# Two experts on two column halves of TensorE: units taken in turn, or matmul by matmul

## The reference, cut to what matters

```python
logits = (t @ w_router + b_router).astype(jnp.float32)
top_logit, top_idx = lax.top_k(logits, TOP_K)          # 4 of 32
...
xb = t_pad[rows]
gu = xb @ w_gate_up[e] + b_gate_up[e]                  # 1024 -> 2048
gate, up = jnp.split(gu, 2, axis=-1)
gate = jnp.minimum(gate, SWIGLU_LIMIT)
up = jnp.clip(up, -SWIGLU_LIMIT, SWIGLU_LIMIT)
act = (up + 1.0) * gate * jax.nn.sigmoid(SWIGLU_ALPHA * gate)
return act @ w_down[e] + b_down[e]                     # 1024 -> 1024
```

## Time and profile before

| what | value |
|---|---|
| median of 3 runs | 1329.62 us (1328.64 to 1331.16) |
| span of the profiled execution | 1325.7 us |
| PE busy | 1273.0 us, 96% |
| PEld busy | 720.2 us, 54% |
| DVE, ACT busy | 256.2 us, 174.9 us |
| read from HBM | 444.80 MB |
| the experts, from the first L657 to the end | 363.2 us to 1325.7 us |

### The profile page before, as it was taken

One profiled execution on the slowest core, in us unless ns is written; L12 is line 12 of the kernel. 1 busy time (PEld: TensorE's weight loads), 2 busy tenths in 40 slices (PEclk: granted clock), 3 DMA queues, 4 the chain that ended last, 5 costly groups with the idle time before them and its releaser, 6 DMA issues.

```text
span 1325.7 us, 14813 instructions
## 1 busy us (share of the span) xinstructions
PE 1273.0 (96%) x5921; PEld 720.2 (54%) x5921; DVE 256.2 (19%) x478; ACT 174.9 (13%) x297; POOL 0.9 (0%) x6
## 2 busy tenths in 40 slices
PE   8999999999899999999999999999999999999997
PEld 6878877888744535353444535353444535353443
DVE  2144221311302202020202202020202202020202
ACT  2233311100201101010101101010101101010100
POOL 0000000000000000000000000000000000000000
PEclk9999999999899999999999999999999999999999
DMA  9622332343698989999999999999999999999994
GB/s 381 259 96 95 112 111 95 130 157 133 264 375 351 367 352 414 420 417 417 418 415 421 414 422 414 420 415 419 418 416 419 415 422 415 421 415 420 416 416 166
DMA packets 78893, 446.29 MB, mean 337 GB/s; under 512 B 6896, under 2 KB 8048, under 8 KB 41232
## 3 DMA queue, kind: packets, MB, share of 16 engines
q1 hardware_dynamic: 78384, 443.64, 82.7%
q10 hardware_dynamic: 480, 2.23, 0.4%
HBM read 444.80 MB, written 1.05 MB: 336 GB/s over the span
## 4 chain that ended last, share of the span: by engine, by line
PE 89%; DVE 7%; issue 2%; ACT 1%; DMA 0%; DVEq 0%
PE ps L657 37%; PE ps L691 22%; PE ps L422 19%; DVE arena L1129 3%; PE ps L700 2%; PE ps L665 2%; DVE arena L1143 1%; DVE arena L1145 1%; DVE arena L1142 1%; ACT arena L898 1%; PE ps L495 1%; PE ps L463 1%; PE ps L431 1%; PE ps L677 0%; PE ps L638 0%
## 5 line engine op out<-in xcount | busy, mean ns | idle before, releaser
L657 PE MATMUL ps<-ring,arena 128*64 128x512 f32 x1984 | 472.4, 598 | 11.4 <-ACT arena L898 10.7
L657 PEld LDWEIGHTS ps<-ring,arena 128*64 128x64 f32 x1984 | 183.7, 136 | 297.9 <-issue 297.4
L691 PE MATMUL ps<-ring,arena 128*64 128x512 f32 x1008 | 285.1, 601 | 22.6 <-DVE arena L1145 22.6
L422 PE MATMUL ps<-arena,ring 128*128 128x256 f32 (+1 forms) x1184 | 268.9, 384 | 1.2 <-DVE arena L1044 1.1
L422 PEld LDWEIGHTS ps<-arena,ring 128*128 128x128 f32 x1184 | 222.0, 190 | 36.5 <-issue 5.0
L691 PEld LDWEIGHTS ps<-ring,arena 128*64 128x64 f32 x1008 | 100.2, 137 | 184.4 <-issue 158.7
L1136 DVE COPY arena<-ps 128x1024 f32<-128x1024 f32 x16 | 19.6, 1225 | 552.9 <-PE ps L657 552.9
L889 ACT ACTIVATE arena<-ps 128x1024 f32<-128x1024 f32 x16 | 16.4, 1024 | 472.6 <-PE ps L657 472.6
L638 PE MATMUL ps<-arena 128*128 128x128 f32 x512 | 63.2, 284 | 1.5 <-DVE arena L1129 1.5
L638 PEld LDWEIGHTS ps<-arena 128*128 128x128 f32 x512 | 60.8, 198 | 5.0 <-issue 5.0
L700 PE MATMUL ps<-arena 128*128 128x256 f32 x256 | 62.0, 386 | 0.0
(11 more groups left out here) (173 smaller groups left out, 493.5 us busy)
## 6 DMA issues: line engine op xcount, KB each, us to landing
ring<-in_w_gate_up SPq DMA_DIRECT2D x248, 1024.0 KB, 13.5
ring<-in_w_down SPq DMA_DIRECT2D x126, 1024.0 KB, 16.9
ring<-in_mix_w SPq DMA_DIRECT2D x37, 1024.0 KB, 4.9
arena<-in_w_gate_up SPq DMA_DIRECT2D x8, 1024.0 KB, 10.1
arena<-in_w_down SPq DMA_DIRECT2D x2, 1024.0 KB, 16.1
arena<-in_consts ACTq DMA_DIRECT2D x1, 1424.0 KB, 13.5
arena<-in_xT SPq DMA_DIRECT2D x2, 544.0 KB, 5.3
out<-arena SPq DMA_DIRECT2D x4, 256.0 KB, 2.6
```

The lines of the kernel that those rows point to most:

```text
L422: last = mm(ps[:, PROJ + half, 0:rhs.shape[-1]], w[:, k, half * P:(half + 1) * P], rhs, start=(k == 0), stop=(k == KC - 1))
L657: last = mm(ps[half, GATE + b], xeT[:, j, half], w[:, b * 512:(b + 1) * 512], start=(j == 0), stop=(j == 7))
L691: last = mm(ps[half, UP + b], e_act[:, k, half], w[:, f * D + b * 512:f * D + (b + 1) * 512], start=(k == 0), stop=(k == 7))
```

## The change

In `gate_up` and `down`, TensorE waits for both experts' units of a block at once, and then goes through the block's matmuls with the two experts alternating: bank 0 of expert 0, bank 0 of expert 1, bank 1 of expert 0, and so on. Each expert's last matmul of the block counts its unit as used. In `down` the count `first_half` moves with the matmul that it hangs on. The number of matmuls, their operands and their sums stay. SP, DVE, ACT and GpSimd have the same instructions in the same order as before.

```diff
-                for q in range(16):
-                    j, x = divmod(q, 2)
-                    w, half = unit_landed(n, q), slice(x * CAP, (x + 1) * CAP)
+                halves = (slice(0, CAP), slice(CAP, 2 * CAP))
+                for j in range(8):
+                    w = [unit_landed(n, 2 * j + x) for x in range(2)]
                     for b in range(4):
-                        last = mm(ps[half, GATE + b], xeT[:, j, half], w[:, b * 512:(b + 1) * 512],
-                                  start=(j == 0), stop=(j == 7))
-                    last.then_inc(units_used, 1)
+                        for x, half in enumerate(halves):
+                            last = mm(ps[half, GATE + b], xeT[:, j, half], w[x][:, b * 512:(b + 1) * 512],
+                                      start=(j == 0), stop=(j == 7))
+                            if b == 3:
+                                last.then_inc(units_used, 1)
...
-                for q in range(16, 24):
-                    if q == 22:
+                halves = (slice(0, CAP), slice(CAP, 2 * CAP))
+                for j in range(8, 12):
+                    if j == 11:
                         turn_weighted(n, last_pair)
-                    j, x = divmod(q, 2)
-                    w, half = unit_landed(n, q), slice(x * CAP, (x + 1) * CAP)
+                    w = [unit_landed(n, 2 * j + x) for x in range(2)]
                     for b in range(2):
                         for f in range(2):
                             k = 2 * (j - 8) + f
-                            last = mm(ps[half, UP + b], e_act[:, k, half],
-                                      w[:, f * D + b * 512:f * D + (b + 1) * 512], start=(k == 0), stop=(k == 7))
-                        if q == 23 and b == 0:
+                            for x, half in enumerate(halves):
+                                last = mm(ps[half, UP + b], e_act[:, k, half],
+                                          w[x][:, f * D + b * 512:f * D + (b + 1) * 512], start=(k == 0), stop=(k == 7))
+                                if b == 1 and f == 1:
+                                    last.then_inc(units_used, 1)
+                        if j == 11 and b == 0:
                             last.then_inc(first_half, 1)
-                    last.then_inc(units_used, 1)
```

## The result

The changed kernel takes 1317.31 us (median of 4 runs, 1316.01 to 1317.51) against 1329.13 us for the kernel before (4 runs, 1327.30 to 1331.16): a ratio of 0.9912, 95% interval 0.9900 to 0.9923, or 11.8 us less. Predicted were 1315.9 us, with a range of 1312.5 to 1321, and 13.7 us less. The profiled execution has a span of 1314.2 us, 11.5 less than before.

The account below looks back on a forecast made before the run. Transfers were taken as the slower side (60.2 us a pair, 0.6 more than TensorE), hidden by a stock of landed units. 10.0 us from earlier landings plus 3.7 from the last pair gave 13.7 less: 1315.9 us, range 1312.5 to 1321.

Parts of the forecast that it names:

- the landings: All later landings of weight units, behind the first pairs, come 10.0 us earlier (bounds 8.7 and 10.7).
- the last pair: Behind its last gate-up unit, the two `down` runs shorten by 2.0 and 1.7 us: 3.7 us less.
- The share of the halves: Alternating halves overlap from start to end: `gate_up` 27.7 us, `down` 10.55 and 3.66, a pair 6.2 us less of TensorE.
- The couple: One matmul of either half, run together: taken as 0.43 us, bounded below by 0.43 and above by 0.49.
- Rivals 1 and 2: Each change of half costs 0.05 us (1327 us, 8%); halves shut each other out (over 500 us slower, 4%).
- The middle pairs: Transfers take 60.2 us a pair, so TensorE's 6.2 us saved become waiting, about 1.3 us a block, worth nothing.
- The first pairs: Transfers stood still for 18.2 us while waiting for TensorE, the most that can come back there.
- The part from TensorE's runs: Shorter runs ahead of pair 1's first `down` unit end the last standstill of transfers 8.7 us earlier.
- the small gaps behind it: Behind the last standstill, up to 482 us, earlier freeing recovers 1.3 us (bounds 0 and 2).
- The slots: SP's 12 slots: freeing units two at a time, up to 1.7 us later, is covered; no new standstill arises.
- Rival 3: TensorE's 1.3 us waits in middle-pair blocks lower the clock to 1.2 GHz: 24 us, 1340 us; chance 5%.
- From span to median: The median of the runs lies 3.9 us above the profiled span, so 1312.0 us becomes 1315.9.

Follow-up runs that it names:

- the loop alone: Only pairs 2 to 14 alternate, the other pairs as in the kernel before: 1329.55 us against 1329.15, ratio 1.0003.
- the last pair alone: Only pair 15 alternates, the other pairs as in the kernel before: 1326.08 us against 1329.15, ratio 0.9975.
- The fill run: The changed kernel with 32 unread matmuls in the idle stretch ahead of the last pair's `down`: 1314.81 us, ratio 0.9897 to the kernel before.
- groups of two: The changed kernel, each expert taking two matmuls (four in the trace) before the other's turn: 1316.86 us, ratio 0.9900 to the kernel before.
- first pairs alone: Only pairs 0 and 1 alternate, the other pairs as in the kernel before: 1321.17 us against 1329.15, ratio 0.9940.
- half bytes, units in turn: The kernel before, with half the bytes in each unit in pairs 2 to 15: 1328.98 us against 1329.85, ratio 0.9991.
- half bytes, alternating: The changed kernel with half the bytes in each unit in pairs 2 to 15: 1228.49 us, ratio 0.9238 to the kernel before.
- other bank: The changed kernel with expert 1 two banks away from expert 0 in `gate_up`: 1317.45 us, ratio 0.9905 to the kernel before.

## Why the prediction was right

**The sum.** The mechanism is the one that was forecast, and each part of it was run by itself. Of the 13.7 us forecast 11.8 were measured; both terms, the landings and the last pair, came out 0.8 to 0.9 us under their forecast in the profiles, and neither by more than such a term varies from profile to profile.

**The share of the halves.** `gate_up` 27.7 predicted, 27.62 and 27.69 measured; `down` 10.55 and 3.66 predicted, 10.52 and 3.58 to 3.65 measured. The couple costs the lower bound, 0.43 us. Rivals 1 and 2 are out: behind the start no couple of 0.48 stands in the rows of pair 0 (64 of them would make `gate_up` 30.9 us), and the bank has no price.

**The middle pairs.** Worth nothing, as predicted, and shown both ways (the loop alone: nothing; the loop with half the bytes: 6.2 us a pair). The starved blocks wait 1.2 to 1.4 us each but for the first one (0.45), 1.3 predicted; `gate_up` is stretched to 34.5 us in the chain's pair 6 (702.67 to 737.19), about 35 predicted.

**The first pairs.** The last landing moved 9.2 us ahead, counted from the first expert matmul; 10.0 was predicted, with bounds of 8.7 and 10.7. The part from TensorE's runs, 8.7, held: counted in the same way, the last standstill ends at 104.0 us before and at 95.2 with the change, 8.8 us earlier. What is left for the small gaps behind it, 1.3 predicted, is 0.4. These profiles don't size that term: with the same first pairs as before, the runs with the loop alone and the last pair alone have their last landing at 941.6 and 942.9, which would make it 0.1 to 1.4. In the 15.2 us behind the standstill the transfers move 358 GB/s before, 375 and 350 in those two runs, and 381 with the change. Single units land over 1 us late there, in both kernels (with the change one lands 3.9 us behind the one ahead of it, where 2.5 is usual); what holds them up stays open.

**The slots.** No new standstill arose (416 GB/s from 470.5 to 523 us); that freeing two units at a time costs nothing fits this, though no run changed it alone. The last standstill ends with the unit issued at 458.9, landed 4.8 later, where before it was 467.2 and 4.7. One sign was set wrong: 418 GB/s "by about 457 us" lies ahead of that standstill's end, which the prediction's own 8.7 us puts at 458.5. The full rate is back from 464 us on.

**The last pair.** 3.7 predicted; 2.8 in the profile, 3.1 (2.0 to 4.7 by the interval) for the last pair alone. At the upper clock the runs shortened as said, by 2.0 and 1.8. The term that came out otherwise is the clock: I kept the 1.7 us that the low level had cost, and it cost 2.35, so the 48 went from 14.19 to 12.87 only. Since this cost varies by itself from 1.4 to 2.9 us (last section), a better price for it could not be had from the one profile before. The fill run takes all of it away.

**Rival 3, the clock in the starved blocks**, did not come: the clock is 1.00 from 523 to 1250 us, also in each 6 us of it, with some 58 waits of up to 1.4 us. Its argument read the idle stretches ahead of `down` a little long: the 22.6 us hold the 4.83 of the last pair, and the others are 1.2 us, not 1.4.

**From span to median.** The spans differ by 11.5 us and the medians by 11.8, so the same distance on both sides was a fair assumption. But a run's time isn't 3.9 us above its own span: in every run on record it is 1.8 us above. The profiled run of the change took 1316.01 us for a span of 1314.2 and was the fastest of four, 1.3 under their median. By the same 1.8 us the profiled run of before took about 1327.5, some 2 under its median of 1329.62. So the 3.9 were 1.8 and a fast run; the forecast held because both profiled runs were fast ones, by nearly the same amount, which is luck.

## What to carry to other kernels

Where two resources are within 1% of each other in each round of a loop, speeding up the one that the chain of waits names moves only the rounds in which the other one still waits for it: look for the stretches where the second stands still (here four windows at 310 to 393 GB/s against 418), and for the work behind its last delivery. Half-width matmuls on different column halves overlap as long as no half is given a longer run than TensorE looks past: groups of two or four matmuls in the trace did; groups of eight lost 1.7 us in each run of matmuls, at its start and end together, and 0.3 to 0.8 more at the changes of unit in the longer runs. Fill a stretch of idle TensorE ahead of matmuls on the path, even with work that nobody reads, if the lowered clock shows behind it (here worth 2.5 us).

## What the runs showed of the hardware that I had not expected

The same idle stretch of 4.8 us ahead of the last `down` costs a different amount from run to run. Over the uninterrupted 12.51 or 10.52 us of the 48 matmuls it was 1.7 us (before), 1.4 (loop alone), 2.2 (first pairs alone), 2.4 (half bytes, units in turn), 2.35 (the change), 2.4 (last pair alone), 2.2 (half bytes, alternating), 2.5 (groups of two, over its own 10.57) and 2.9 (other bank), and nothing with the stretch filled. Units in turn lie at 1.4 to 2.4, alternating ones at 2.2 to 2.9. The ranges overlap and each form varies by 0.7 us or more, so the order of the matmuls is not all of it; whether it is a part isn't settled by these nine profiles. So a price read from one profile for such a drop holds to about a microsecond and not better, which is 0.1% of this kernel.
